# Split an expert table in two and gather its halves with separate indirect transfers

## The chip, the cores and the metric

The kernel runs on one core of one Trainium2 chip. The metric is device time of one execution in microseconds (us); the kernel before takes 2918.26 us (median of 3 runs, 2916.95 to 2922.1).

## The reference

Two transformer blocks run one after the other on one sequence of 512 tokens of width 1024, all in float32. The change lies in the last layer of the second block, a mixture of very small experts. Each of 16,384 experts is one pair of vectors of 1024 numbers: a down vector `u` and an up vector `v`. Each token picks 16 experts in each of 8 heads.

```
def peer(h, w_query, keys_1, keys_2, expert_u, expert_v):
...
    def chunk_fn(hc):
...
        top_s, pos = lax.top_k(cand, PEER_TOPK)
        experts = jnp.take_along_axis(cand_idx, pos, axis=-1)
        gate = jax.nn.softmax(top_s.astype(jnp.float32), axis=-1).astype(hc.dtype)
        u = jnp.take(expert_u, experts, axis=0)
        act = jax.nn.gelu(jnp.einsum('chkd,cd->chk', u, hc))
        v = jnp.take(expert_v, experts, axis=0)
        return jnp.einsum('chk,chkd->cd', gate * act, v)
```

## The kernel before

Every engine has its own program, written out by hand, and they meet at semaphores. The 512 tokens are four tiles of 128. The first 1572 us are the first block and the dense part of the second; nothing of them is touched. The expert layer follows. It runs through 32 steps (`STEPS`: 4 tiles times 8 heads) of 16 rows each (`TOPK`), 512 rows `g` in all. In row `g`, each of the 128 partitions holds the chosen expert of its own token.

- **GpSimd (POOL)** issues one indirect DMA for each row (L1662). It reads 128 expert numbers from a column of `ecur` and brings 128 table rows of 8 KB, `u` and `v` side by side, into slot `g % RING` of `ring_e`, a ring of 10 slots in the `arena`. For a step's first row it waits for `ecur_ready`, and from row 10 on for `rows_used`, which says that TensorE is done with the slot. Nothing else stands on this queue in this stage.
- **VectorE (DVE)** waits for the row's own semaphore `row_landed`, and forms the dot product of `u` with the token's vector (`row_dot`, L1581). This is a custom instruction that reads two operands in SBUF, and it writes the product over `u`. Between two dots it does one of 16 pieces of routing for the step after next (`route`): these find the top 16 of the candidates and end with `ecur`.
- **ScalarE (ACT)** takes the dots two at a time (`weigh_pair`): Gelu (L1041), the gate (L1045), and two diagonal matrices `diag` (L1047, L1049).
- **TensorE (PE)** multiplies each diagonal by the `v` half of its slot, two matmuls of 128x512 a row, accumulated over a tile's 128 rows in PSUM (`row_pair`; matmuls are recorded at L415), and adds 1 to `rows_used` after each row.
- Between rows of the first tile TensorE also does the query projections and key scores of the steps to come, whose weights come on SyncE's queue in rows of 4 KB. At the end of each tile its sum is turned and added to `x` (`turn_tile`, `add_tile`).

The ring is what couples the engines: a slot's journey is issue, DMA queue, transfer, dot, weighing, matmul, release, and there are 10 slots.

The `v` half lies behind the `u` half in a slot (elements `D` to `2D`). The one semaphore of a row says that both have landed.

Of the kernel before, what the change touches and what calls it, by code (L numbers as in the profile page):

```python
# [20 lines left out]
D = 1024  # L21
# [82 lines left out]
def build(nc, a, out):  # L104
    ctx = ExitStack()
    with ctx:
# [214 lines left out]
        pm_ready = sem("pm_ready")  # L321
        pn_ready = sem("pn_ready")
        pool_done = sem("pool_done")
        pool_seen = sem("pool_seen")
        pq_done = sem("pq_done")
        prep_done = sem("prep_done")
        prep_ps = sem("prep_ps")
# [30 lines left out]
        ug_ready = sem("ug_ready")  # L358
        uw_done = sem("uw_done")
        vc_ready = sem("vc_ready")  # L360
        vec_seen = sem("vec_seen")
        vec_step = sem("vec_step")
        vnew_ready = sem("vnew_ready")
        w_ready = sem("w_ready")
# [10 lines left out]
        slot_ready = [sem(f"slot{j}_ready") for j in range(SLOTS)]  # L375
        slot_a_ready = [sem(f"ada_slot{j}_ready") for j in range(SLOTS)]
        slot_2_ready = [sem(f"ada_2_slot{j}_ready") for j in range(SLOTS)]
        row_landed = [sem(f"expert_row{j}_ready") for j in range(RING)]

        block = ctx.enter_context(nc.Block())  # L380

# [31 lines left out]
        def _(pe):  # L413
# [316 lines left out]
            def row_pair(p, start, stop):  # L730

                pe.wait_ge(diag_ready, p + 1)
                c = p // (HEADS * SB)
                for k in range(BATCH):
                    r = (p * BATCH + k) % RING
                    for v in range(2):
                        ins = mm(PS[:, 4 * (c % 2) + v, :], diag[:, p % NB, k, :],
                                 ring_e[:, r, D + v * S:D + (v + 1) * S],
                                 start and k == 0, stop and k == BATCH - 1)
                    ins.then_inc(rows_used, 1)  # L740
# [366 lines left out]
        def _(dve):  # L1107
# [386 lines left out]
            def route(r, j):  # L1494
# [25 lines left out]
                elif j == 5:  # L1520
                    copy(idf, icur[:]).then_inc(vec_step, 1)
                    tt(cand.rearrange("p (x y) -> p x y", y=16), last(vcur[:, 0, :], 16), mid(vcur[:, 1, :], 16), ADD).then_inc(vec_step, 1)
                    n(vec_step), n(vec_step)
                elif j == 6:
                    V.max(tcur[:, 0:8], cand).then_inc(vec_step, 1)
                    n(vec_step)
                elif j == 7:
                    V.max_index(pcur[:, 0:8], tcur[:, 0:8], cand).then_inc(vec_step, 1)
                    n(vec_step)
                elif j == 8:  # L1530
                    V.match_replace(s2, tcur[:, 0:8], cand, NEG).then_inc(vec_step, 1)
                    n(vec_step)
                elif j == 9:
                    V.max(tcur[:, 8:16], s2).then_inc(vec_step, 1)
                    n(vec_step)
                elif j == 10:
                    V.max_index(pcur[:, 8:16], tcur[:, 8:16], s2).then_inc(vec_step, 1)
                    n(vec_step)
                elif j == 11:
                    V.tensor_scalar(pab[:, 0, :], pcur[:], 4, None, ALU.logical_shift_right).then_inc(vec_step, 1)  # L1540
                    V.tensor_scalar(pab[:, 1, :], pcur[:], 15, None, ALU.bitwise_and).then_inc(vec_step, 1)
                    n(vec_step), n(vec_step)
                elif j == 12:
                    copy(ifl, pab[:]).then_inc(vec_step, 1)
                    n(vec_step)
                    settled()
                    tt(eqv, last(ifl, 16), mid(iota, 2, 16), ALU.is_equal).then_inc(vec_step, 1)
                    n(vec_step)
                elif j == 13:
                    tt(eqv, eqv, idf.unsqueeze(2).to_broadcast([P, 2, 16, 16]), MUL).then_inc(vec_step, 1)  # L1550
                    n(vec_step)
                elif j == 14:
                    V.tensor_reduce(sel.rearrange("p z k -> p (z k)"), eqv.rearrange("p z k x -> p (z k) x"), X, ADD).then_inc(vec_step, 1)
                    n(vec_step)
                else:
                    stt(exf, sel[:, 0, :], float(NKEYS), sel[:, 1, :], MUL, ADD).then_inc(vec_step, 1)
                    n(vec_step)
                    if r >= 3:
                        dve.wait_ge(w_ready2, (r - 2) * TOPK)
                    tt(gcur[:, r % 3, :], tcur, tcur[:, 0:1].to_broadcast([P, 16]), SUB).then_inc(sm_in, 1)  # L1560
                    settled()
                    copy(ecur[:, r % 2, :], exf).then_inc(ecur_ready, 1)

            def gate_sum(r):
# [73 lines left out]
        def _(pool):  # L1638
# [17 lines left out]
            for r in range(STEPS):  # L1656
                pool.wait_ge(ecur_ready, r + 1)
                for j in range(TOPK):
                    g = r * TOPK + j
                    if g >= RING:  # L1660
                        pool.wait_ge(rows_used, g - RING + 1)
                    nc.gpsimd.indirect_dma_start(  # L1662
                        out=ring_e[:, g % RING, :], out_offset=None, in_=a["experts"],
                        in_offset=bass.IndirectOffsetOnAxis(ap=ecur[:, r % 2, j:j + 1], axis=0)
                    ).then_inc(row_landed[g % RING], 16)


def tiles_of(w):
# [50 lines left out]
def layout(i):  # L1719
# [20 lines left out]
    order = np.array([0, 1, 2, 3, 4, 8, 5, 9, 6, 10, 7, 11] + list(range(12, 28)))  # L1740
    a["w_in_2"] = np.ascontiguousarray(tiles_of(g["w_in_2"][0])[order])
    a["branch"] = np.ascontiguousarray(np.concatenate([tiles_of(g["pool_up_2"][0]), tiles_of(g["conv_out_2"][0])], 2))
    a["experts"] = np.concatenate([g["expert_u_2"][0], g["expert_v_2"][0]], 1)
    m = np.zeros((P, NMATS), np.float32)
    for n, v in (("w2k", g["cmp_k_w2"][0]), ("w2v", g["cmp_v_w2"][0]), ("keys1", g["sub_keys_1_2"][0].T),
                 ("keys2", g["sub_keys_2_2"][0].T), ("poolw", g["pool_w_2"][0].transpose(1, 0, 2).reshape(P, -1))):
# [43 lines left out]
```

## Time and profile before

| | |
|---|---|
| median of 3 runs | 2918.26 us |
| profiled execution's own time | 2921.43 us |
| its span, first to last instruction | 2919.7 us |
| mean granted TensorE clock, of full speed | 0.938 |
| busy: PE, DVE, ACT, POOL | 2474.1, 1579.5, 677.9, 597.0 us |
| moved by the GpSimd queue | 587.24 MB in 87,552 packets |
| first indirect issue to last | 1572.4 to 2877.2 us |

The busy times are over the whole span. The expert layer is its last 1350 us, and there each engine stands differently than in the mean, so the views are read by stretches of time. "DMA share" is the mean busy share of the core's 16 DMA engines. The records of packets overlap a little, so that it can read 1.01.

### The profile page before, as it was taken

Reading aid. Unit: us, or ns where it says so; the run is one execution under the profiler, and the core shown is the slowest. Engines: PE = TensorE matmul, PEld = TensorE weight load, DVE = VectorE, ACT = ScalarE, POOL = GpSimd, SP = SyncE. Lnnn points to the kernel's source line nnn. Section 1 sums busy time; section 2 is a strip of 40 time slices with the busy share of each in tenths; the row PEclk is TensorE's granted clock in tenths of the full one; section 3 lists DMA queues with packets and bytes.
Section 4 is the critical chain, followed back from the end, with each engine's and each line's share of the span. In section 5 each row is a group of like instructions: output and inputs, shape, how many; then the busy total and the mean of one; then the engine's idle time right before and its main releaser. Section 6 shows DMA issues by size and latency. Waiting matters only on the chain.

```text
span 2919.7 us, 21725 instructions
## 1 busy us (share of the span) xinstructions
PE 2474.1 (85%) x6738; PEld 1189.6 (41%) x6738; DVE 1579.5 (54%) x3290; ACT 677.9 (23%) x1886; POOL 597.0 (20%) x612
## 2 busy tenths in 40 slices
PE   4998697788999999899898999787777777777776
PEld 3442496653444454344344444233333323232233
DVE  4731774433665500357314666667666766667664
ACT  2112121312010000211102333333333333333332
POOL 1100000000000000000001444444444444344441
PEclk7998696799999989999899999999999999999999
DMA  6541001012443311122124899999999999999995
GB/s 243 187 151 36 0 0 36 22 58 87 165 155 139 136 60 65 57 79 72 49 74 194 352 407 404 421 421 421 421 421 420 421 422 421 403 421 422 421 421 243
DMA packets 115590, 682.61 MB, mean 234 GB/s; under 512 B 12446, under 2 KB 16542, under 8 KB 49708
## 3 DMA queue, kind: packets, MB, share of 16 engines
q0 software_dynamic: 87552, 587.24, 49.4%
q1 hardware_dynamic: 27948, 94.29, 9.4%
q8 instruction: 42, 0.69, 0.1%
q14 instruction: 48, 0.39, 0.0%
HBM read 679.39 MB, written 2.10 MB: 233 GB/s over the span
## 4 chain that ended last, share of the span: by engine, by line
PE 50%; DMA 25%; DVE 5%; ACT 4%; issue 1%; POOL 1%; DVEq 0%; ACTq 0%; POOLq 0%
PE PS L415 49%; DMA arena<-experts_dram,ecur 25%; DVE arena L1581 2%; DVE arena L1112 1%; ACT arena L1045 1%; POOL arena L1662 1%; ACT L1041 1%; ACT const L1049 0%; ACT const L1047 0%; DVE arena L1359 0%; DVE rs L1165 0%; ACT arena L1041 0%; PE PS L628 0%; DVE arena L1118 0%; DVE arena L1115 0%
## 5 line engine op out<-in xcount | busy, mean ns | idle before, releaser
L415 PE MATMUL PS<-arena,const 128*128 128x512 f32 (+1 forms) x2076 | 981.1, 620 | 279.8 <-ACT const L1049 262.1
L1581 DVE CUSTOM_DVE_ANT_0 arena<-arena 128x1024 f32<-128x1024 f32 x512 | 627.4, 1225 | 422.0 <-DMA arena<-experts_dram,ecur 420.5
L1662 POOL DMA_INDIRECT arena<-experts_dram,ecur x512 | 546.0, 1066 | 1349.0 <-PE PS L415 735.0
L415 PE MATMUL PS<-hT,ring 128*128 128x512 f32 x1792 | 784.6, 597 | 22.7 <-ACT hT L832 22.0
L415 PEld LDWEIGHTS PS<-arena,const 128*128 128x128 f32 x2076 | 390.6, 196 | 852.1 <-issue 434.5
L415 PEld LDWEIGHTS PS<-hT,ring 128*128 128x128 f32 x1792 | 341.8, 192 | 449.9 <-issue 444.3
L415 PE MATMUL PS<-arena,ring 128*128 128x512 f32 (+1 forms) x864 | 352.4, 574 | 18.5 <-ACT arena L999 11.5
L415 PEld LDWEIGHTS PS<-arena,ring 128*128 128x128 f32 x864 | 170.0, 215 | 201.0 <-issue 183.6
L1041 ACT ACTIVATE arena<-arena 128x2 f32<-128x2 f32 x256 | 51.8, 202 | 711.1 <-DVE arena L1581 710.7
L415 PE MATMUL PS<-arena 128*128 128x128 f32 (+2 forms) x1216 | 182.0, 314 | 23.3 <-DVE arena L1112 8.7
L415 PEld LDWEIGHTS PS<-arena 128*128 128x128 f32 x1216 | 166.3, 215 | 42.2 <-issue 17.3
L1118 DVE SCALAR_TENSOR_TENSOR xT<-PS,mod,xT 128x128 f32<-128x128 f32 (+1 forms) x56 | 29.2, 522 | 273.6 <-PE PS L415 265.3
L1112 DVE TENSOR_TENSOR arena<-arena 128x16 f32<-128x16 f32 (+6 forms) x190 | 98.4, 518 | 97.0 <-ACT arena L976 48.9
L1118 DVE SCALAR_TENSOR_TENSOR arena<-arena,silc 128x512 f32<-128x512 f32 (+1 forms) x168 | 126.3, 752 | 12.7 <-DMA arena<-ada_dram 7.0
L1045 ACT ACTIVATE arena<-arena 128x1 f32<-128x1 f32 x512 | 122.8, 287 | 8.6
L1115 DVE TENSOR_SCALAR arena<-PS,param 128x512 f32<-128x512 f32 x56 | 44.6, 797 | 134.0 <-PE PS L415 130.7
L824 ACT ACTIVATE sq<-xT 128x512 f32<-128x512 f32 x32 | 20.1, 630 | 368.6 <-PE PS L415 202.2
L1118 DVE SCALAR_TENSOR_TENSOR arena<-PS,param,arena 128x511 f32<-128x511 f32 (+2 forms) x124 | 92.9, 749 | 14.4 <-DVE arena L1115 1.8
L1047 ACT ACTIVATE const<-const,arena 128x128 f32<-128x128 f32 x256 | 98.8, 386 | 0.0
L1049 ACT ACTIVATE const<-const,arena 128x128 f32<-128x128 f32 x256 | 98.7, 386 | 0.0
L415 PE MATMUL PS<-sq,const 128*128 128x512 f32 (+2 forms) x174 | 70.2, 555 | 30.0 <-ACT sq L824 14.8
L1647 POOL DMA_DIRECT2D arena<-ada_dram x4 | 2.1, 528 | 452.0 <-ACT arena L950 452.0
(171 smaller groups left out, 1335.0 us busy)
## 6 DMA issues: line engine op xcount, KB each, us to landing
arena<-ada_dram POOLq DMA_DIRECT2D x96, 512.0 KB, 5.0
ring<-w_in_dram SPq DMA_DIRECT2D x52, 512.0 KB, 3.5
ring<-up_dram SPq DMA_DIRECT2D x44, 512.0 KB, 3.5
ring<-down_dram SPq DMA_DIRECT2D x16, 704.0 KB, 4.0
ring<-w_out_dram SPq DMA_DIRECT2D x16, 512.0 KB, 3.5
ring<-query_dram SPq DMA_DIRECT2D x16, 512.0 KB, 5.6
arena<-experts_dram,ecur POOLq DMA_INDIRECT x512
ring<-cmp_dram SPq DMA_DIRECT2D x8, 512.0 KB, 3.5
```

Of the source, the lines that this page charges most:

```text
L415: return nc.tensor.matmul(o, l, r, start=start, stop=stop)
L824: A(sq[:, k % 2, :], xT[:, k, :], ACT.Square).then_inc(sq_ready, 1)
L1041: A(wts[:, b, :], dots[:, b, :], ACT.Gelu_apprx_tanh).then_inc(gelu_ready, 1)
L1045: A(wts[:, b, k:k + 1], wts[:, b, k:k + 1], ACT.Copy, scale=gcur[:, r % 3, j:j + 1]).then_inc(w_ready2, 1)
L1047: A(diag[:, b, 0, :], ident, ACT.Copy, scale=wts[:, b, 0:1]).then_inc(act_step, 1)
L1049: A(diag[:, b, 1, :], ident, ACT.Copy, scale=wts[:, b, 1:2]).then_inc(diag_ready, 1)
L1112: return V.tensor_tensor(out=o, in0=x, in1=y, op=op)
L1115: return V.tensor_scalar(o, x, s1, s2, op0, op1)
L1118: return V.scalar_tensor_tensor(out=o, in0=x, scalar=s_, in1=y, op0=op0, op1=op1)
L1581: V.tensor_tensor_reduce(out=u, in0=u, in1=hrow[:, (r // HEADS) % 2, :], scale=1.0, scalar=0.0, op0=MUL, op1=ADD, accum_out=dots[:, p % NB ...
L1647: pool.dma_start(ring_2[:, j, :], a["ada_2"][j]).then_inc(slot_2_ready[j], 16)
L1662: nc.gpsimd.indirect_dma_start(out=ring_e[:, g % RING, :], out_offset=None, in_=a["experts"], in_offset=bass.IndirectOffsetOnAxis(ap=ecur[ ...
```

## The change

The table `experts` (16,384 rows of 8 KB) becomes two tables, `expert_u` and `expert_v` (rows of 4 KB). For each row `g` GpSimd issues two indirect DMAs with the same indices, the `u` half first, each with a semaphore of its own in each slot: `row_landed` for `u`, the new `v_landed` for `v`. VectorE's dot waits for `u` alone. TensorE waits for `v` before a row's matmuls. The bytes that are moved stay the same, and so do the ring and the order of the rows.

```
         row_landed = [sem(f"expert_u{j}_ready") for j in range(RING)]
+        v_landed = [sem(f"expert_v{j}_ready") for j in range(RING)]
...
                 for k in range(BATCH):
-                    r = (p * BATCH + k) % RING
+                    g = p * BATCH + k
+                    r = g % RING
+                    pe.wait_ge(v_landed[r], 16 * (g // RING + 1))
...
                     settled()
+                    if r >= 2:
+                        for g in range((r - 2) * TOPK, (r - 1) * TOPK):
+                            dve.wait_ge(v_landed[g % RING], 16 * (g // RING + 1))
                     copy(ecur[:, r % 2, :], exf).then_inc(ecur_ready, 1)
...
                     nc.gpsimd.indirect_dma_start(
-                        out=ring_e[:, g % RING, :], out_offset=None, in_=a["experts"],
+                        out=ring_e[:, g % RING, :D], out_offset=None, in_=a["expert_u"],
                         in_offset=bass.IndirectOffsetOnAxis(ap=ecur[:, r % 2, j:j + 1], axis=0)
                     ).then_inc(row_landed[g % RING], 16)
+                    nc.gpsimd.indirect_dma_start(
+                        out=ring_e[:, g % RING, D:], out_offset=None, in_=a["expert_v"],
+                        in_offset=bass.IndirectOffsetOnAxis(ap=ecur[:, r % 2, j:j + 1], axis=0)
+                    ).then_inc(v_landed[g % RING], 16)
```

The first place is GpSimd's queue at the head of the expert layer, where it turned to the gathers. Before, from the last instructions of the loop that loads the modulation weights (`x9` is nine such rows one after the other):

```order
L1648 COMPARE_AND_BRANCH
L1662 DMA arena<-experts_dram,ecur 128x2048 [waits ecur_ready]
L1662 DMA arena<-experts_dram,ecur 128x2048 x9
L1662 DMA arena<-experts_dram,ecur 128x2048 [waits rows_used] x6
L1662 DMA arena<-experts_dram,ecur 128x2048 [waits rows_used,ecur_ready]
L1662 DMA arena<-experts_dram,ecur 128x2048 [waits rows_used] x15
```

After the change, on the same engine, from the last row of the ring's first filling to the second step's first row:

```order
L1666 DMA arena<-expert_u_dram,ecur 128x1024
L1670 DMA arena<-expert_v_dram,ecur 128x1024
L1666 DMA arena<-expert_u_dram,ecur 128x1024 [waits rows_used]
L1670 DMA arena<-expert_v_dram,ecur 128x1024
...
L1666 DMA arena<-expert_u_dram,ecur 128x1024 [waits rows_used,ecur_ready]
L1670 DMA arena<-expert_v_dram,ecur 128x1024
```

Each issue has become two, 1024 instead of 2048 elements in a partition, and only the first of the two waits. The queue holds 1024 gathers where it held 512.

The second place is VectorE at the end of a step, where `ecur` of the step after next is written. Before (the ISA rows are the dot and the reading of its accumulator):

```order
L1553 TENSOR_REDUCE arena<-arena 128x32 [waits vec_step]
L1581 ISA arena<-arena 128x1024 [waits expert_row1_ready]
L1581 ISA arena 128x1
L1118 SCALAR_TENSOR_TENSOR arena<-arena 128x16 [waits vec_step]
L1112 TENSOR_TENSOR arena<-arena 128x16 [waits w_ready2]
L1121 CAST ecur<-arena 128x16 [waits vec_step]
L1581 ISA arena<-arena 128x1024 [waits expert_row2_ready]
```

After, at the same place:

```order
L1554 TENSOR_REDUCE arena<-arena 128x32 [waits vec_step]
L1585 ISA arena<-arena 128x1024 [waits expert_u1_ready]
L1585 ISA arena 128x1
L1119 SCALAR_TENSOR_TENSOR arena<-arena 128x16 [waits vec_step]
L1113 TENSOR_TENSOR arena<-arena 128x16 [waits w_ready2]
L1122 CAST ecur<-arena 128x16 [waits expert_v4_ready,expert_v3_ready,expert_v5_ready,expert_v2_ready,expert_v6_ready,expert_v1_ready,expert_v7_ready,expert_v0_ready,expert_v8_ready,expert_v9_ready,vec_step]
L1585 ISA arena<-arena 128x1024 [waits expert_u2_ready]
```

No instruction has moved. The cast that gives GpSimd its next numbers now also waits until the `v` halves of the step just done, its last row among them, have landed, since those transfers read the `ecur` that it overwrites. On TensorE the matmul rows stand as before, and the first matmul of each row names `expert_v`*n*`_ready` as a further wait.

## Rows read from the trace of the kernel before

**Rows 1.** Windows: busy us (instructions) by engine, clock, DMA share, GB/s
```profile
1572.00:1600.00 28.00, 28.00 (x91) 14.37 (x90) 10.11 (x40) 5.78 (x10) 9.46 (x10) 1.00 0.94 380
1600.00:1700.00 100.00, 96.70 (x257) 45.33 (x256) 64.88 (x172) 36.67 (x117) 37.76 (x33) 1.00 0.91 366
1700.00:1800.00 100.00, 100.00 (x264) 46.70 (x263) 63.59 (x161) 34.33 (x112) 42.45 (x40) 1.00 0.99 398
1800.00:1900.00 100.00, 75.41 (x167) 30.61 (x166) 68.97 (x178) 34.95 (x114) 44.65 (x40) 0.96 1.01 422
1900.00:2880.00 980.00, 750.64 (x1634) 301.97 (x1634) 661.98 (x1641) 321.98 (x1078) 411.68 (x390) 0.97 1.01 420
```

**Rows 2.** Chain that ended last, in time order, from 1995 to 2030 us
```profile
2001.95 1.25 DVE arena L1581 x2
...
2004.57 3.71 PE PS L415 x8
...
2008.55 18.23 DMA arena<-experts_dram,ecur
...
2026.80 1.24 DVE arena L1581 x2
```

**Rows 3.** DMA view, 2000 to 2200 us: gathers alone
```profile
DMA packets 11569, 84.26 MB, mean 421 GB/s; under 512 B 1286, under 2 KB 1286, under 8 KB 1286
```

**Rows 4.** DMA view, 38 to 44 us: weights in rows of 4 KB
```profile
DMA packets 679, 2.45 MB, mean 408 GB/s; under 512 B 82, under 2 KB 82, under 8 KB 679
```

**Rows 5.** Windows of 2 us in that stretch, columns as in Rows 1
```profile
38.00:40.00 2.00, 0.01 (x1) 0.00 (x0) 1.97 (x2) 0.00 (x0) 0.00 (x0) 0.50 1.00 401
40.00:42.00 2.00, 0.00 (x0) 0.00 (x0) 1.90 (x4) 0.00 (x0) 0.00 (x0) 0.50 1.05 420
```

**Rows 6.** The issuing line: its group on the page, then 1700 us to the end
```profile
L1662 POOL DMA_INDIRECT arena<-experts_dram,ecur x512 | 546.0, 1066 | 1349.0 <-PE PS L415 735.0
```
```profile
L1662 POOL DMA_INDIRECT arena<-experts_dram,ecur x470: 932/937/1993, 1699.4 to 2877.2; - x157
```

**Rows 7.** Timeline of POOL while the ring fills: start, us, [idle before <-releaser]
```profile
1574.94 0.94 POOL L1662 DMA_INDIRECT arena<-experts_dram,ecur  x1 [0.30 <-issue]
1576.18 0.94 POOL L1662 DMA_INDIRECT arena<-experts_dram,ecur  x1 [0.30 <-issue]
```

**Rows 8.** Timeline of POOL, 2060 to 2069 us
```profile
2061.27 0.94 POOL L1662 DMA_INDIRECT arena<-experts_dram,ecur  x1 [1.56 <-PE PS L415]
2062.99 1.62 POOL L1662 DMA_INDIRECT arena<-experts_dram,ecur  x1 [0.78 <-PE PS L415]
2064.92 0.94 POOL L1662 DMA_INDIRECT arena<-experts_dram,ecur  x1 [0.30 <-issue]
```

**Rows 9.** Timeline of DVE, the same stretch: dots
```profile
2062.58 1.23 DVE L1581 CUSTOM_DVE_ANT_0 arena<-arena 128x1024 f32<-128x1024 f32 x1 [0.70 <-DMA arena<-experts_dram,ecur]
...
2065.06 1.22 DVE L1581 CUSTOM_DVE_ANT_0 arena<-arena 128x1024 f32<-128x1024 f32 x1 [0.83 <-DMA arena<-experts_dram,ecur]
```

**Rows 10.** Waits from 1700 to 2880 us: in total, times, longest
```profile
POOL arena L1662 <- PE PS L415: 660.8, 423, 8.7
```

**Rows 11.** The page's GB/s in 40 equal slices of 73 us
```profile
GB/s 243 187 151 36 0 0 36 22 58 87 165 155 139 136 60 65 57 79 72 49 74 194 352 407 404 421 421 421 421 421 420 421 422 421 403 421 422 421 421 243
```

**Rows 12.** Timeline of all engines at the end of a step
```profile
2008.27 0.17 DVE L1121 CAST ecur<-arena 128x16 uint32<-128x16 f32 x1
...
2009.40 1.23 DVE L1581 CUSTOM_DVE_ANT_0 arena<-arena 128x1024 f32<-128x1024 f32 x1 [0.96 <-DMA arena<-experts_dram,ecur]
...
2009.54 3.70 PE L415 MATMUL PS<-arena,const 128*128 128x512 f32 x8 [1.26 <-ACT const L1049]
```

**Rows 13.** Chain that ended last, at the end of the gathers
```profile
2877.19 18.13 DMA arena<-experts_dram,ecur
...
2895.34 1.24 DVE arena L1581 x2
...
2897.96 5.49 PE PS L415 x24
```

More of the change, by code:

```diff
@@ L323, in build @@
         pool_done = sem("pool_done")
-        pool_seen = sem("pool_seen")
         pq_done = sem("pq_done")
@@ L360, in build @@
         vc_ready = sem("vc_ready")
-        vec_seen = sem("vec_seen")
         vec_step = sem("vec_step")
@@ L377, in build @@
         slot_2_ready = [sem(f"ada_2_slot{j}_ready") for j in range(SLOTS)]
-        row_landed = [sem(f"expert_row{j}_ready") for j in range(RING)]
+        row_landed = [sem(f"expert_u{j}_ready") for j in range(RING)]
+        v_landed = [sem(f"expert_v{j}_ready") for j in range(RING)]
         block = ctx.enter_context(nc.Block())
@@ L1742, in layout @@
     a["branch"] = np.ascontiguousarray(np.concatenate([tiles_of(g["pool_up_2"][0]), tiles_of(g["conv_out_2"][0])], 2))
-    a["experts"] = np.concatenate([g["expert_u_2"][0], g["expert_v_2"][0]], 1)
+    a["expert_u"], a["expert_v"] = np.ascontiguousarray(g["expert_u_2"][0]), np.ascontiguousarray(g["expert_v_2"][0])
     m = np.zeros((P, NMATS), np.float32)
```

## The prediction

> **What bounds the kernel now.** Read the windows first [rows 1]. From 1800 to 2880 us the DMA share stands at 1.01 and the rate at 420 to 422 GB/s, while TensorE is busy 77% (750.64 of 980 us), VectorE 68% and GpSimd 42%. The 16 DMA engines have no idle time left in that stretch; every other engine has. The chain of waits says the same: of each turn of the ring of 25 us, some 18 us are the wait for a gather to land [rows 2]. At 421 GB/s [rows 3] a row of 128 x 8192 B = 1.0486 MB takes 2.49 us, so those 18 us are mostly seven older rows in the DMA queue, and not latency. The dots start when a row lands, 2.48 us apart [rows 9]. Ahead of 1800 us it is otherwise: in the first tile the query projections keep TensorE busy 97 to 100%, and the DMA share is 0.91, then 0.99.
>
> So the price of this change is read from what a row costs the DMA engines, and then from whether GpSimd can still feed them.
>
> **DMA: the same bytes in packets of half the size.** Before, a row is 128 packets of 8 KB and 16 small ones for the semaphore: in [rows 3] 1286 of 11,569 packets are under 512 B, one in nine. After, it is 256 packets of 4 KB and 32 small ones. No gather of 4 KB rows is in the trace, but weights in rows of 4 KB are, and at 38 to 44 us two queues of them keep the DMA engines as full: 679 packets, 82 of them small, all others under 8 KB, 408 GB/s [rows 4]. At 408 GB/s a row takes 2.57 us, 0.08 us more than 2.49. In single windows of 2 us there the rate is 401 and 420 GB/s at shares of 1.00 and 1.05 [rows 5]. These are my bounds: 2.50 us (+0.01) and 2.615 us (+0.125). I take the mean over the stretch, since it is the longest full one of such packets.
>
> The Trainium skill ("DMA: Bandwidth & Descriptors", Why small descriptors are slow) gives a cost for each packet of about 3 cycles beside one cycle for each 32 B, and a little metadata. By that rule 4 KB packets would cost 1.2 to 1.5% more than those of 8 KB, an estimate from the page of +14 to +18 us here. The rows say 421/408, or 3.2%, and the sum goes by them.
>
> How many rows pay it? 470 of the 512 issues start after 1699 us [rows 6]. The 42 before fall where the DMA engines idle: 9% of 100 us are 9 us against 33 x 0.08 = 2.6 us, so they pay nothing. Without that cover it would be 42 x 0.08 = 3.4 us. The 40 rows from 1700 to 1800 us find 1% idle, 1 us. That makes 470 x 0.08 - 1 = **+36.6 us**.
>
> **GpSimd: two issues for one.** While the ring fills, issues stand back to back: 0.94 us and a gap of 0.30, 1.24 us each [rows 7], and two are 2.48 us a row against the DMA engines' 2.57. That leaves almost nothing, and issues are not always 0.94 us: the mean is 1.066 [rows 6]. The long ones have one look. The issue at 2062.99 took 1.62 us: a dot ran from 2062.58 to 2063.81, and the issue ended 0.80 us after it [rows 8, 9]. An issue that starts during a dot is held until the dot ends and then needs 0.8 us; one that starts first isn't held, as at 2064.92, 0.14 us before the next dot.
>
> From that I work out whether GpSimd keeps up when it is behind. Dots come every 2.57 us and last 1.23. An issue held until a dot's end is done 0.81 us later; the next starts 1.11 us after the dot's end, and the next dot only 2.57 - 1.23 = 1.34 us after it. So this second issue goes through in 0.94 us, and the third starts 2.35 us after the dot's end, within the next dot, and is held to its end. Two issues for each dot: just enough. I put the steady state at **0**. The margin is 0.23 us, and what is once lost isn't regained while the dots come at that pace.
>
> Where is it lost? At the end of a tile TensorE frees no slot for up to 8.7 us [rows 10] and then several at once. Now GpSimd refills at 1.24 us a row, twice as fast as the DMA engines drain. Even so the slice at 2482 to 2555 us shows 403 GB/s for 421 [rows 11], 4.3% of 73 us = 3.1 us lost at the third boundary, and none at the other two. With 2.48 us a row the queue isn't refilled, so I let all three boundaries lose that: **+6 us**. Bounds: 0, and 3 x 8.7 = 26 us.
>
> **The new waits.** A wait already satisfied costs GpSimd nothing that shows: the gap of 0.30 us stands at 2064.92 too, where the instruction has one [rows 7, 8]. VectorE's cast into `ecur` now waits for the last `v` of the step. In a full queue that `v` lands 1.3 us after its `u`, about when the dot of 1.23 us ends, and VectorE idles 0.96 us before the next dot [rows 12]. Behind the cast stands that dot; if the cover is gone, 32 casts at up to 1.3 us are 42 us at most. TensorE's wait for `v`: its matmuls start over 2.5 us after a pair's second dot begins (2001.95 to 2004.57, [rows 2]), `v` is there, and TensorE idles 1.26 us before a pair [rows 12]. Only up to 1800 us has it no idle time: some 75 rows, at 0.05 us each below 4 us. I take 0 for all of these.
>
> **The gain.** The last dot waits for the last `u` and no longer for the last byte: the chain there is transfer, dot from 2895.34, matmuls from 2897.96 [rows 13], and the dot starts half a row earlier, **-1.3 us**. At the head, the first dots wait for nothing that a gather brings late. Within the full stretch an earlier `u` only frees slots sooner, and the queue is seven rows deep already.
>
> **Sum**: 2921.4 (the profiled execution's own time) + 36.6 + 0 + 6 + 0 - 1.3 = 2962.7 us. That execution lies 3.2 us above the median of 2918.3, so the forecast for a median is **2960 us**.
>
> **Rivals.**
> - *GpSimd becomes the bound.* For it: 2 x (1.066 + 0.30) = 2.73 us a row from the means as they are [rows 6, 7], 0.24 more than 2.49: + 470 x 0.24 = 113 us, **3030 us**. If issues and dots met at random, 1.23 of 2.57 us would find a dot running with 0.61 us still to go, 0.29 us for each issue, 2 x (1.24 + 0.29) = 3.06 us a row: +268 us, 3186 us. Against it: the two fall into step as worked out, and a held issue is held only because it would otherwise be early. It decides once an issue takes more than 2.57/2 - 0.30 = 0.985 us in the mean without the hold being such spare time. The Trainium skill ("SBUF — State Buffer", Who interferes with whom) has the rule: a VectorE instruction with two SBUF inputs contends with a GpSimd instruction that reads SBUF, and the second to start is blocked. The trace agrees, 1.62 us for 0.94.
> - *No change.* 4 KB packets run at the 420 GB/s of the better window and GpSimd keeps up: 470 x 0.01 = 5, less 1.3: **2922 us**. For it: two windows of 2 us are little to tell 401 from 420.
> - *Faster.* The dot starts 1.3 us earlier after its issue, slots turn sooner, and the DMA idle time up to 1800 us (6% of 28, 9% of 100, 1% of 100: 12 us) goes with the 1.3 us at the end: **2905 us**. It needs packets of 4 KB at no cost, as above; and there TensorE, busy 97 to 100%, is the bound. An earlier `u` doesn't help it.
>
> The skill's rules for kernel authors on the same DMA page advise one large transfer over several. Its fit of about 2 us fixed for each DMA would add 2 us a row if nothing overlapped; rows landing 2.48 us apart show that it overlaps.
>
> **Chances.** My forecast, the packets' price with GpSimd in step: 0.50. GpSimd the bound: 0.35. No change: 0.10. Faster: 0.05. A measurement of this kernel can tell 0.2%, about 6 us, so the first two are slower (0.85). The range goes from 2930, which leaves out the last two, to 3130, into the upper part of the first rival; the forecast's own cases, from the better bound to the worse (470 x 0.125 = 59 us), lie between 2925 and 2985.
>
> **What would show it.** After the change, from 1800 us on: DMA share still 1.00 to 1.01 at 408 GB/s, dots 2.57 us apart, GpSimd busy 80% and more with issues of 0.94 and about 1.05 us in turn, and VectorE's idle time still ended by the gather of `u`. If the share falls below 0.97 while GpSimd's idle time before an issue is 0.30 us throughout and no longer ended by TensorE, GpSimd is the bound. If the rate is 420, the packets cost nothing. The forecast fails above all if the step of two issues a dot is lost in places and not found again, or if the cast's wait holds VectorE.

## The result and the profile after

The changed kernel takes 3100.64 us (median of 4 runs, 3096.23 to 3103.57) against 2919.22 us before (2916.95 to 2922.1, 4 runs beside them): ratio 1.062, 95% interval 1.0601 to 1.0638. That is slower, by 181 us where 41 were forecast.

The windows of the kernel after, with the columns of [rows 1]:

```profile
1600.00:1700.00 100.00, 96.70 (x252) 45.17 (x251) 63.22 (x169) 35.80 (x114) 63.34 (x62) 0.98 0.88 330
1700.00:1800.00 100.00, 93.19 (x238) 42.52 (x237) 58.95 (x149) 30.75 (x101) 72.41 (x68) 0.98 0.97 365
1800.00:1900.00 100.00, 73.64 (x154) 30.69 (x153) 57.74 (x145) 27.78 (x94) 75.11 (x71) 0.91 0.96 364
1900.00:3050.00 1150.00, 819.62 (x1668) 333.68 (x1666) 676.55 (x1686) 331.65 (x1107) 859.54 (x793) 0.89 0.97 363
```

From 1900 us on the DMA share is 0.97 and the rate 363 GB/s, where 1.00 at 408 was forecast. So two things are off: the DMA engines have gaps, and even at a full share the rate would be 363/0.97 = 374 GB/s. GpSimd is busy 75% and does 793 issues in 1150 us, 2.90 us a row.

The page of the kernel after: the DMA rate in 40 slices of 77 us, and the two issuing lines:

```profile
GB/s 230 199 134 21 0 0 55 1 82 156 156 155 140 56 70 54 75 75 55 54 236 381 361 379 347 372 364 362 374 334 371 353 378 362 362 349 373 356 372 271
...
L1666 POOL DMA_INDIRECT arena<-expert_u_dram,ecur x512 | 513.8, 1004 | 828.9 <-DVE ecur L1122 587.1
...
L1670 POOL DMA_INDIRECT arena<-expert_v_dram,ecur x512 | 588.3, 1149 | 156.0 <-issue 155.4
```

Where [rows 11] holds 421, slice after slice, the rate now goes up and down between 334 and 381. The two issues of a row take 1.004 + 1.149 us in the mean and 0.30 in front of each, 2.75 us. At first sight this is the rival in which GpSimd is the bound, with its 2.73 us a row. The waits say that this isn't all. Waits of the kernel after, 1700 to 3050 us (in total, times, longest); "remote" stands where no record of a signal explains the release:

```profile
POOL arena L1666 <- remote: 40.2, 20, 4.5
POOL arena L1666 <- PE PS L414: 38.9, 44, 6.9
ACT arena L1058 <- remote: 33.7, 4, 17.6
ACT arena L1018 <- remote: 25.6, 3, 11.6
DVE xT L1119 <- remote: 17.9, 4, 6.7
DVE arena L1571 <- issue: 15.6, 2, 15.3
```

The trace of the kernel before has no wait that ends with "remote" in this stretch. One such place, timeline of the kernel after in the last step but one of the second tile:

```profile
2284.30 1.04 PE L725 MATMUL PS<-const,hT 128*128 128x128 f32 x8
...
2298.29 0.60 ACT L1058 ACTIVATE arena<-PS 128x512 f32<-128x512 f32 x1 [17.58 <-remote]
...
2303.36 0.16 DVE L1571 RECIPROCAL arena<-arena 128x1 f32<-128x1 f32 x1 [15.28 <-issue]
...
2305.99 3.78 PE L414 MATMUL PS<-arena,const 128*128 128x512 f32 x4 [20.65 <-ACT const L1050]
```

TensorE's eight transposes, which turn the token rows of the next tile (`turn_rows`), begin at 2284.30 and take 1.04 us of work. ScalarE, whose next work waits for them alone, copies their result 13 us later. VectorE then waits for ScalarE and TensorE for both, and the three stand for 15 to 21 us. GpSimd has the same at smaller scale, 20 times up to 4.5 us.

### The profile page after: what moved, and what is told of

It is laid out like the page before. It is cut to its first block, busy times and chain, and to the rows that moved or that the text cites. A ratio compares the mean times of both kernels' runs of the same rounds, so it can differ in the third digit from the quotient of the medians.

```text
span 3094.5 us, 22733 instructions
## 1 busy us (share of the span) xinstructions
PE 2534.9 (82%) x6738; PEld 1216.9 (39%) x6738; DVE 1578.0 (51%) x3290; ACT 677.5 (22%) x1886; POOL 1153.4 (37%) x1124
## 4 chain that ended last, share of the span: by engine, by line
PE 52%; POOL 12%; issue 11%; DVE 4%; DMA 3%; another core or an unknown queue 2%; ACT 2%; POOLq 0%; DVEq 0%; ACTq 0%
PE PS L414 51%; POOL arena L1670 6%; POOL arena L1666 5%; DMA arena<-expert_u_dram,ecur 3%; DVE arena L1585 1%; DVE arena L1113 1%; ACT arena L1046 0%; DVE arena L1360 0%; DVE rs L1166 0%; PE PS L627 0%; ACT const L1050 0%; DVE xT L1119 0%; ACT const L1048 0%; DVE arena L1119 0%
## 5 line engine op out<-in xcount | busy, mean ns | idle before, releaser
L414 PE MATMUL PS<-arena,const 128*128 128x512 f32 (+1 forms) x2076 | 1044.3, 656 | 392.5 <-issue 260.8
L1666 POOL DMA_INDIRECT arena<-expert_u_dram,ecur x512 | 513.8, 1004 | 828.9 <-DVE ecur L1122 587.1
L414 PEld LDWEIGHTS PS<-arena,const 128*128 128x128 f32 x2076 | 419.7, 209 | 999.5 <-issue 849.3
L1670 POOL DMA_INDIRECT arena<-expert_v_dram,ecur x512 | 588.3, 1149 | 156.0 <-issue 155.4
L1651 POOL DMA_DIRECT2D arena<-ada_dram x4 | 2.1, 530 | 447.3 <-ACT arena L951 447.3
L1656 POOL DMA_DIRECT2D arena<-ada_dram x44 | 23.3, 530 | 333.3 <-DVE arena L1119 333.3
L1048 ACT ACTIVATE const<-const,arena 128x128 f32<-128x128 f32 x256 | 98.8, 386 | 0.0
```

The source lines that it names most:

```text
L414: return nc.tensor.matmul(o, l, r, start=start, stop=stop)
L1048: A(diag[:, b, 0, :], ident, ACT.Copy, scale=wts[:, b, 0:1]).then_inc(act_step, 1)
L1656: pool.dma_start(ring_2[:, j, :], a["ada_2"][bass.ds(i * SLOTS + j, 1)].rearrange("o p n -> p (o n)")).then_inc(slot_2_ready[j], 16)
L1666: nc.gpsimd.indirect_dma_start(out=ring_e[:, g % RING, :D], out_offset=None, in_=a["expert_u"], in_offset=bass.IndirectOffsetOnAxis(ap=ecu ...
L1670: nc.gpsimd.indirect_dma_start(out=ring_e[:, g % RING, D:], out_offset=None, in_=a["expert_v"], in_offset=bass.IndirectOffsetOnAxis(ap=ecu ...
```

## The experiments

All times are medians, and each ratio is taken against the kernel before, run on the same occasion. The experiments fell on six occasions after the first result. The kernel before stood at 2917.8 to 2919.8 us on all of them. The changed kernel did not: unedited, it has two levels.

| changed kernel, unedited | us | range, runs | ratio, interval |
|---|---|---|---|
| the result | 3100.64 | 3096.23 to 3103.57, 4 | 1.062, 1.0601 to 1.0638 |
| `r_after_again` | 2964.06 | 2949.45 to 2973.39, 4 | 1.014, 1.0101 to 1.0179 |
| `r_after_third` | 2962.57 | 2954.2 to 2976.5, 4 | 1.0157, 1.0121 to 1.0192 |
| `r_after_fourth` | 2969.35 | 2955.08 to 2991.35, 6 | 1.0177, 1.0146 to 1.0208 |
| `r_after_fifth` | 3091.89 | 3089.04 to 3101.93, 5 | 1.0593, 1.0578 to 1.0607 |
| `r_after_sixth` | 3085.65 | 3078.66 to 3113.02, 4 | 1.0607, 1.0556 to 1.0658 |

On one occasion all runs of it stand at one level. I call them the lower (2963 to 2969) and the upper (3086 to 3101). Every interval lies above 1, but only the upper level is more than 2% slower beyond doubt. The expectations of the first four experiments (`e_one_operand`, `e_v_plain`, `e_extra_gather`, `e_one_signal`) took 3100 us for the kernel's only time. Their occasion was of the lower level, so what an edit took away there is counted from some 2965 us.

### On occasions of the lower level

**`e_one_operand`: take away what holds an issue.**

```
-                V.tensor_tensor_reduce(out=u, in0=u, in1=hrow[:, (r // HEADS) % 2, :], ...
+                V.tensor_reduce(dots[:, p % NB, g % BATCH:g % BATCH + 1], u, X, ADD).then_inc(dots_ready, 1)
```

> The changed kernel, but VectorE's dot is a plain sum over u (one operand in SBUF, nothing written over u) in place of the product with the token's vector, so the output is not the reference's; issues, packets, signals and waits are as in the changed kernel. If a gather's issue is held by the two-operand dot and GpSimd is the bound: every issue takes 0.94 us, a row costs GpSimd 2.48 us, the DMA engines become the bound at 2.57 us a row, and the kernel takes about 2960 us. If the time comes from something else (packets, waits for v, late signals), issues may get shorter but the time stays within 30 us of 3100.

Measured: 2946.47 us (2945.02 to 2949.81), ratio 1.0099 (1.0082 to 1.0116), 21 us below `e_one_signal` on the same occasion (2967.86). Windows of it, then its issues from 1900 to 2850 us (count; busy us, mean ns; idle before):

```profile
1900.00:2850.00 950.00, 713.24 (x1547) 287.20 (x1545) 630.93 (x1232) 309.26 (x1028) 698.62 (x740) 0.96 1.03 409
```
```profile
L1668 POOL DMA_INDIRECT arena<-expert_v_dram,ecur x370 | 350.1, 946 | 113.1 <-issue 112.8 <-PE PS L414 0.3
L1664 POOL DMA_INDIRECT arena<-expert_u_dram,ecur x370 | 349.9, 946 | 138.6 <-issue 93.8 <-PE PS L414 44.8
```

With a dot of one SBUF operand the issues take 0.946 us in the mean, GpSimd waits for slots again, and the DMA engines run full at 409 GB/s.

**`e_one_operand_before`: the same edit in the kernel before**, as the control.

> The kernel before (one gather of 8 KB a row) with a dot that only sums u, so that it reads one operand in SBUF and leaves the product with the token out. It is the control to the same edit in the changed kernel (2946 us). If the hold of an issue by a dot costs the kernel before nothing, since its GpSimd waits for slots anyway, the time stays within 0.2% of 2919 us, and the issues' mean falls from 1.07 to 0.94 us. If the dot's own length or the hold cost something there too, it comes out 5 us or more below, and the packets' price in the changed kernel is larger than 27 us by that much.

Measured: 2914.8 us (2913.84 to 2917.39, 10 runs), ratio 0.9987 (0.9978 to 0.9996); the issues' mean is 952 ns. The dot's form is worth 3.8 us there. Between the two kernels with the short dot lie 2946.47 - 2914.8 = 31.7 us (two occasions, the kernel before at 2918.29 and 2918.61 us). With hardly an issue held in either, this is what the packets (and whatever else a second issue costs) amount to: 0.067 us for each of 470 rows.

**`e_v_plain` and `e_v_sync`: one gather a row, the packets as in the change.** The first lets GpSimd bring `v` in a plain DMA, the second SyncE.

```
+                    pool.dma_start(ring_e[:, g % RING, D:], a["expert_v"][(g % 128) * P:(g % 128 + 1) * P]
+                                   ).then_inc(v_landed[g % RING], 16)
```

> The changed kernel, but the v half comes by a plain DMA from GpSimd's queue of 128 fixed table rows of 4 KB (no indices; output not the reference's). Bytes, packets of 4 KB, number of transfers and their signals and waits are the same; a plain issue took 0.53 us in the trace of before. If GpSimd's issuing is the bound: 0.53 + 0.30 + 1.0 + 0.30 = 2.1 to 2.2 us a row, below the DMA engines' 2.57; about 2960 us with the DMA share at 1.0. If packets of 4 KB or the doubled signals are what costs, it stays near 3100 us.

Measured: 2950.29 us (2948.91 to 2952.44), ratio 1.0111 (1.0094 to 1.0128), 408 GB/s. The expectation's 1.0 us for the indirect issue was a miss: it took 1.57 us in the mean, mostly held by a dot and done 0.85 us after the dot's end. With 0.56 us for the plain issue GpSimd still kept up.

> The changed kernel, but the v half comes by a plain DMA on SyncE's queue of 128 fixed table rows of 4 KB, issued row by row as slots come free (the last four query weight blocks are issued between them; output not the reference's). GpSimd issues one gather a row, as before the change; packets of 4 KB, transfers and signals are as many as in the changed kernel, and the early dot is kept. If only the packets cost: 2.57 us a row and 2945 to 2955 us. If the early dot or the many signals slow the kernel by themselves: 3000 us and more.

Measured: 2950.87 us (2949.11 to 2952.12), ratio 1.0112 (1.0095 to 1.0128), 408 GB/s. Both say 32 us for the packets, with dots as they are and GpSimd, in `e_v_sync`, as idle as in the kernel before. In both, `v` comes from fixed table rows and not from chosen ones.

**`e_extra_gather`: the second gather without small table rows.**

```
-                        out=ring_e[:, g % RING, :D], out_offset=None, in_=a["expert_u"],
+                        out=ring_e[:, g % RING, :], out_offset=None, in_=a["experts"],
...
-                        out=ring_e[:, g % RING, D:], out_offset=None, in_=a["expert_v"],
+                        out=spare[:, g % RING, :], out_offset=None, in_=a["extra"],
```

> The gather of before (8 KB rows, one transfer) plus a second gather of 16 B per token with the same indices into a spare buffer that nobody uses (its signal is waited for as v's is). Two gathers and two signals a row, but the bytes come in packets of 8 KB. If GpSimd's issuing is the bound: as slow as the changed kernel, 3070 to 3110 us, with the DMA share clearly below 1. If packet size is what costs: about 2925 us (the 128 small packets add little).

Measured: 2958.23 us (2956.84 to 2958.48), ratio 1.0134 (1.0117 to 1.0151). Neither theory had that: 40 us with packets of 8 KB kept, far from GpSimd as the bound. Its second gather moves only 2 KB a row. Its window from 1900 us:

```profile
1900.00:2850.00 950.00, 716.73 (x1534) 289.63 (x1535) 631.35 (x1596) 304.48 (x1017) 728.09 (x729) 0.95 1.01 404
```

The DMA engines have no idle time here, and yet they move 404 GB/s where the kernel before moves 420. In nearly all stretches of 40 us outside the spells described below it is 404 to 411, as with rows of 4 KB (409 in most stretches of `e_v_sync`). Both kernels have 288 packets a row where the kernel before has 144. So most of the price is one for the number of packets and not for the size of a table row: 128 packets of 16 bytes and 16 for the signal cost here what splitting 128 packets in two costs there. The expectation's "the 128 small packets add little" was wrong.

**`e_one_signal`: the new waits and the early dot taken back.** Both halves add to one semaphore, the dot waits for both, and TensorE and the cast no longer wait for `v`.

> The changed kernel, but both halves count on one semaphore and the dot waits for both (32 instead of 16); TensorE and the cast into ecur no longer wait for v. Tells what the separate signal and its waits cost or bring. If the waits for v on TensorE or on VectorE's cast are part of the loss: 10 to 60 us below 3100. If issuing is the bound: the ring loses only 1.3 us of lead per row and the time stays at 3100 within 15 us.

Measured: 2967.86 us (2964.45 to 2972.4), ratio 1.0167 (1.015 to 1.0184), the same as the changed kernel at its lower level (2963 to 2969, on other occasions). So the separate signals cost and bring nothing that shows beside those 7 us.

**`r_after_again`: the changed kernel unedited.**

> The changed kernel itself, word for word, once more, on the chip and beside the kernels of this call. The first four experiments with the same 1024 issues took 2946 to 2968 us, the changed kernel 3100; its trace has semaphore updates of TensorE that reach their waiters up to 13 us late, and theirs do not. If that belongs to the kernel (its early dot meeting the issues), it is again 3090 to 3110 us with issues of 1.08 us in the mean. If it belongs to where it was run, it is 2950 to 2975 us here.

Measured: 2964.06 us. Its trace shows what GpSimd's two issues cost when nothing else disturbs. Its issues from 2190 to 2300 us, then from 2304 to 2483 us:

```profile
L1666 POOL DMA_INDIRECT arena<-expert_u_dram,ecur x42 | 44.8, 1067 | 12.8 <-issue 11.9 <-PE PS L414 0.9
L1670 POOL DMA_INDIRECT arena<-expert_v_dram,ecur x43 | 40.3, 936 | 13.1 <-issue 12.5 <-PE PS L414 0.6
```
```profile
L1670 POOL DMA_INDIRECT arena<-expert_v_dram,ecur x65 | 76.4, 1176 | 19.8 <-issue 19.8
L1666 POOL DMA_INDIRECT arena<-expert_u_dram,ecur x64 | 63.8, 997 | 19.5 <-issue 17.1 <-PE PS L414 2.4
```

And the windows of it, one in step and the two that hold the spells out of step (2304 to 2483 and 2648 to 2827 us), with one between them:

```profile
1900.00:2300.00 400.00, 299.38 (x658) 120.67 (x657) 265.09 (x669) 127.14 (x429) 306.05 (x309) 0.97 1.02 405
2304.00:2483.00 179.00, 134.42 (x265) 53.59 (x266) 114.87 (x288) 55.28 (x183) 139.84 (x129) 0.90 1.00 380
2490.00:2640.00 150.00, 115.97 (x261) 47.76 (x260) 98.38 (x249) 47.30 (x160) 114.51 (x117) 0.95 1.02 407
2648.00:2827.00 179.00, 129.56 (x264) 51.67 (x262) 114.30 (x287) 53.98 (x180) 140.06 (x128) 0.92 0.99 377
```

In step, one of the two issues is 1.067 us and the other 0.936: two for each dot, as worked out. Out of step both are held at times, 1.176 + 0.997 + 0.60 = 2.77 us a row, and the rate is 380 and 377 GB/s for 406: 179 x (1 - 380/406) + 179 x (1 - 377/406) = 24 us lost. How a spell looks, timeline of GpSimd and the dots:

```profile
2659.78 2.28 DVE L1119 SCALAR_TENSOR_TENSOR xT<-PS,mod,xT 128x128 f32<-128x128 f32 x6
...
2662.64 1.21 DVE L1585 CUSTOM_DVE_ANT_0 arena<-arena 128x1024 f32<-128x1024 f32 x1
2662.70 1.96 POOL L1670 DMA_INDIRECT arena<-expert_v_dram,ecur  x1 [0.30 <-issue]
...
2664.19 1.22 DVE L1585 CUSTOM_DVE_ANT_0 arena<-arena 128x1024 f32<-128x1024 f32 x1
2664.96 1.26 POOL L1666 DMA_INDIRECT arena<-expert_u_dram,ecur  x1 [0.30 <-issue]
...
2665.68 1.21 DVE L1585 CUSTOM_DVE_ANT_0 arena<-arena 128x1024 f32<-128x1024 f32 x1
2666.53 1.17 POOL L1670 DMA_INDIRECT arena<-expert_v_dram,ecur  x1 [0.30 <-issue]
```

The first line is the last six of the eight instructions of `add_tile`, which adds the finished tile's sum to `x`. In all they take VectorE 3.05 us, from 2659.01, and rows land meanwhile. The dots then stand 1.5 us apart, since VectorE catches up with them, and three issues in a row are held, each to 0.8 us after a dot's end (2663.85 + 0.81 = 2664.66). The forecast's two issues a dot took dots at even distances.

The seven traces of the lower level with two gathers a row and the long dot (`r_after_again`, `r_after_third`, `r_after_fourth`, `e_one_signal`, `e_v_first`, `e_one_table`, `e_extra_gather`) all have `add_tile` at 2314 to 2321 us and again at 2652 to 2665. From 2280 to 2320 us their rate is 402 to 409 GB/s, from 2320 to 2360 it is 372 to 383; from 2680 to 2720 it is 368 to 392. `e_one_operand` has `add_tile` too, at 2311 and 2643 us, and there the rate stays at 410. So a spell needs issues that dots can hold, and it begins where `add_tile` has bunched the dots. The first `add_tile`, near 1984 us, brings a smaller fall or none, and no run leaves `add_tile` out. How long a spell lasts differs, from some 40 us in `r_after_third` to some 180 here.

**`e_v_first`: `v` issued before `u`**, so that the dot is late instead of early.

> The changed kernel with the two issues of a row exchanged: v first, then u. The dot now waits for the row's last byte, as before the change, and v is always there. Issues, packets, signals are the same. If what GpSimd loses above the packets' 2.57 us a row is a matter of where the dots fall between the issues: still 2950 to 2975 us, with stretches of steps at 2.56 us and others at 2.75 us a row. If the early dot is what brings dots and issues out of step: 2950 us throughout.

Measured: 2971.35 us (2963.29 to 2974.88), ratio 1.0175 (1.0152 to 1.0197), beside `r_after_third`:

> The changed kernel itself a third time. It took 3100 us in the first comparison and 2964 us (2949 to 2973) in the second, with the kernel before at 2919 both times. If the first was a matter of that place or time, this is 2945 to 2975 us again, without late semaphore updates. If the kernel has two ways to run, 3100 us can come back, here or within the rounds.

at 2962.57 us. The rate falls at the same places. The order of the halves is no cause of the spells.

**`e_more_signals`: `e_v_sync` with three more tiny transfers a row**, since the upper level's trace shows late signals:

```
+                for x in range(3):
+                    sp.dma_start(spare[0:16, g % RING, x, :], a["extra"][0:16]).then_inc(v_landed[g % RING], 16)
```

> The kernel with v by SyncE's plain DMAs, and behind each of them three tiny ones (16 x 16 B) on the same semaphore, which TensorE and the cast wait for with 64 in place of 16 (output not the reference's). A row has five transfers' signals in place of the changed kernel's two and the kernel before's one; GpSimd has one issue a row. If many signals are what makes semaphore updates arrive late: well above 3000 us, with updates of TensorE late in the trace. If not: 2950 to 2990 us.

Measured: 2980.77 us (2979.3 to 2982.22), ratio 1.0209 (1.0192 to 1.0226), no wait that ends with "remote". The 96 small packets that a row has more than in `e_v_sync` go with 30 us (2980.77 - 2950.87, two occasions), and signals in number make none late, at least on an occasion of the lower level.

**`r_after_fourth`, and `e_one_table`: the table not split**, its rows 2e and 2e + 1 gathered.

```
-                        in_offset=bass.IndirectOffsetOnAxis(ap=ecur[:, r % 2, j:j + 1], axis=0)
+                        in_offset=bass.IndirectOffsetOnAxis(ap=ecur[:, r % 2, TOPK + j:TOPK + j + 1], axis=0)
```

> The changed kernel once more, nothing edited, with five rounds. Of four medians of it so far one stood at 3100 us and the later ones at 2964 and 2963. If the 3100 us are a place or a time and not the kernel's, as I now hold, it comes out at 2955 to 2975, issues of 1.00 to 1.04 us in the mean, TensorE's semaphore updates at the end of the matmul. If the kernel itself has such a way of running, so that it should come back now and then, 3090 to 3110, with DMA share near 0.97 at 363 GB/s and updates up to 13 us late.

> The changed kernel, but the table isn't split: u and v of an expert stand side by side as before, and the two gathers of a row read the 4 KB rows 2e and 2e+1 of it (VectorE writes 32 numbers a step instead of 16, in two instructions where one stood). If what a row costs more comes from the packets' size and GpSimd's two issues alone, 2955 to 2975 us, as the changed kernel beside it. If it comes from where the halves stand in the memory (two tables, each with its own region), most of it goes, 2925 to 2940 us.

The first expectation counts one median too many: there were three. Measured: 2969.35 us, and 2972.71 us (2963.9 to 2984.07), ratio 1.0193 (1.0175 to 1.021). Where the halves stand in memory makes no difference that shows at the lower level.

### On occasions of the upper level

**`r_after_fifth` and `r_one_operand_again`.** Their chip is the one on which `e_one_operand` and `e_one_signal` had stood at the lower level.

> The changed kernel again, on whatever chip it falls to, with its one-operand form beside it. If 3100 us belong to a place, most places give 2955 to 2975 us, issues near 1.02 us in the mean and about 1.01 of DMA share at 396 to 400 GB/s; where 3100 comes back, the neighbour on the same chip tells what it rests on. If the first result was a rare event of one loading, it is 2955 to 2975 us here too.

> The changed kernel with a dot that only sums u (one operand in SBUF), as once before, beside the unchanged one. On a place where the changed kernel runs at 2960 us: 2944 to 2952. On a place where it runs at 3100: 2944 to 2952 as well if all the loss there comes from held issues; 3000 to 3030 if signals that come late stop the ring there whatever the dot reads.

Measured: 3091.89 us for the changed kernel, and 3072.44 us (3069.19 to 3082.78) with the short dot, ratio 1.0532 (1.0511 to 1.0553); that is more than the expectation had for late signals. Waits of the latter, 1700 us to the end:

```profile
POOL arena L1664 <- PE PS L414: 125.9, 53, 5.5
...
POOL arena L1664 <- remote: 56.8, 20, 5.1
...
ACT arena L1018 <- remote: 35.2, 4, 11.9
DVE xT L1119 <- remote: 23.6, 3, 11.9
```

Hardly an issue is held in it, they take 0.94 us in the mean, and GpSimd waits 183 us for slots (54 in `e_one_operand`, to 2850 us); still 126 us of the loss stay (3072.44 - 2946.47). Its DMA rate from 2000 to 2200 us, in slices of 5 us:

```profile
GB/s 415 405 407 412 177 347 393 416 410 303 362 418 409 377 266 312 384 415 413 410 409 410 208 326 382 417 410 410 410 410 303 245 333 403 417 410 410 410 406 206
```

`e_one_operand` holds 406 to 411 in every slice of the same stretch. Here the engines reach that rate too, and most of the loss lies in six stops. The hold is worth 19.5 us here (3091.89 - 3072.44) and 16 to 23 at the lower level (2962.57 to 2969.35, less 2946.47). So the upper level isn't the time that dots hold GpSimd's issues: it is 126 us of something else, on top.

**`r_after_sixth`, `r_v_sync_again`, `r_extra_again`, one after the other on one chip.** The count in the first expectation is one too many: there were three low medians of the unedited kernel, and the fourth is that of `e_one_signal`, which is also the low one on the same chip.

> The changed kernel once more, as the measure for three others beside it. Of six medians so far two stood at 3092 and 3101 us and four at 2963 to 2969 (one of the low ones and one of the high ones on the same chip, so it isn't the chip). I expect one of the two again, 2955 to 2975 or 3085 to 3105, and nothing between; the three others tell what the high one rests on only if it comes.

> As e_v_sync: v comes by SyncE's plain transfers from fixed rows, and GpSimd issues one gather a row (the sum is over other rows of v). Where the changed kernel stands at 2965, 2951 as before. Where it stands at 3100: 2951 as well if the late signals come from GpSimd's second gather of each row, 3060 or more if they come from the doubled number of packets and landing signals, which this kernel has too.

> As e_extra_gather: u and v in one gather of 8 KB rows, and a second gather of 16 B rows into a buffer that nobody reads, waited for as v is. Where the changed kernel stands at 2965, 2958 as before. Where it stands at 3100: 3060 or more if the late signals come from the second gather, 2958 if they need packets of 4 KB.

Measured: 3085.65 us; 2952.19 us (2950.59 to 2954.92), ratio 1.012 (1.0103 to 1.0136); and 3099.21 us (3088.84 to 3106.22), ratio 1.061 (1.0586 to 1.0634). Waits of `r_v_sync_again`, 1700 to 2900 us:

```profile
POOL arena L1676 <- PE PS L424: 675.0, 420, 8.7
...
POOL arena L1676 <- issue: 19.7, 46, 2.2
```

And of `r_extra_again`:

```profile
POOL spare L1671 <- issue: 124.5, 408, 0.4
POOL arena L1667 <- issue: 106.0, 348, 0.3
POOL arena L1667 <- PE PS L415: 62.0, 47, 13.1
ACT arena L1059 <- remote: 56.1, 5, 21.6
```

With all of the change's packets and landing signals but one gather a row, the time is that of the lower level (2950.87 in `e_v_sync`, the same kernel), and no wait from 1700 us on ends with "remote"; one of 2.1 us does before, the only one in a trace with one gather a row. With the table's rows left at 8 KB and a second gather of 16 bytes a partition, the upper level is there in full, ScalarE's wait for the transposes of token rows up to 21.6 us. `e_extra_gather` is the same kernel at 2958.23 us. So the upper level needs an occasion on which it can come, and on this one it came with GpSimd's second gather of each row; packets of 4 KB aren't needed for it, and with doubled landing signals alone it didn't come.

## Why the prediction was wrong

**What failed** is the step "GpSimd: two issues for one", where the prediction put "the steady state at 0". The second gather of each row on GpSimd costs 133 us at the upper level (3085.65 - 2952.19, against as many packets with one gather), and about 13 at the lower (2964.06 - 2950.87). The recorded result stands at the upper level, 140 us above the forecast. At the lower level the forecast of 2960 us is 3 to 9 us low, and that is partly luck: it had some 5 us too many for packets and too few for what stands behind the tile boundaries.

The prediction also took the DMA queue to stay "seven rows deep". With two issues a row it doesn't: in `r_after_again` a gather lands 6.6 us after its issue (median, on its page), in `e_v_sync` 18.1. Before the change a pause of GpSimd or of a slot was covered by the queue; after it, little is.

**The likely rival was not it either.** GpSimd as the bound had 3030 us, from 2.73 us a row, and the trace's 2.75 looks like it. But a row took 2.90 us, and with the hold gone the upper level keeps 126 us of its loss (`r_one_operand_again`). The longer issues in that trace are mostly not what sets its pace. The rival's second price has an error of its own: an issue that a dot holds for 0.61 us and then needs 0.81 is 0.48 us longer than 0.94, not 0.61. That makes 2.94 us a row and some 3130 us in place of 3186.

**DMA packets, +36.6 us.** Slightly large: 31.7 us with the short dot in both kernels, 32 with one gather a row, at the 408 GB/s that was forecast and a share of 1.02. The forecast tied it to the packets' size; `e_extra_gather` ties most of it to their number. The estimate from the Trainium skill ("DMA: Bandwidth & Descriptors", Why small descriptors are slow) was 14 to 18 us; the rows of weights were the better guide.

**In step.** Right as a mechanism: 1.067 and 0.936 us in turn for the forecast's 1.05 and 0.94. "What is once lost isn't regained while the dots come at that pace" was wrong in its second half: in `r_after_again` spells end after some 180 us. The hold is there with a dot of two SBUF operands and gone with one, 0.946 us. That is as the Trainium skill has it ("SBUF — State Buffer", Who interferes with whom). The short dot also writes nothing over `u`, and no run tells the two apart. All of it is worth about 19 us.

**Tile boundaries, +6 us.** Mis-sized, and for another reason than the one given. The loss isn't TensorE's pause at the boundary but the spells behind it: in `r_after_again` TensorE turns the second tile's sum at 2308 us and the third's at 2651, `add_tile` follows at 2316 and 2659, and the spells with it. They cost 24 us in that profile, within the bounds of 0 to 26.

**New waits, 0.** Right at the lower level: `e_one_signal` has none of them and is no faster. At the upper level it was not tried.

**The gain, -1.3 us.** Too small to be seen. Taking the early dot away (`e_one_signal`, `e_v_first`) changed nothing measurable.

**What stays open** is what the upper level is made of. Shown is where it shows: signals that engines wait for come many us late and part of their records is missing. It came with two gathers a row on GpSimd, on 3 of 7 occasions, and not by the chip alone; that it stays away with one rests on `r_v_sync_again`, on one occasion, and on the kernel before, on all of them. Not told apart are the second gather as such and a GpSimd that is left without spare time (675 us of waiting in `r_v_sync_again`, 62 in `r_extra_again`); `e_v_plain`, with one gather, one plain transfer and 70 us of waiting for slots in 950, ran only at the lower level. Nor is it known why, with the long dot, packets take longer there even at a full share (363/0.97 = 374 GB/s against 396/1.01 = 392).

## What to carry to other kernels

Where a DMA queue is the bound, splitting its transfers costs the packets' price (some 3% of a row from 144 to 288 packets here) and then whatever the issuing engine runs into: count its time per row against the bound, and treat a margin of a few per cent as none. An issue that is held behind another engine's work stays in step only while that work comes evenly, and a queue that was deep before is thin once its issuer is near its limit. And a time from one occasion may be a level and not the kernel's only one: repeat a surprising one elsewhere, with a neighbour that lacks the suspect, before explaining it.

## What the runs showed of the hardware

- An indirect gather of 128 rows that isn't held occupies GpSimd for 0.94 to 0.95 us, with 0.30 us ahead of it where issues stand back to back, whether the rows are 8 KB, 4 KB or 16 bytes. One that starts within a dot of two SBUF operands, written over one of them, ends 0.8 us after it; beside sums of one operand the mean is 0.946 us.
- At a full DMA share the expert rows came at 421 GB/s with 144 packets a row and at about 409 with 288, whether the packets were 4 KB long or half of them 8 KB and half 16 bytes.
- The same kernel had two levels 4% apart, each steady over all runs of an occasion, while the kernel before stood at 2918 to 2920 us beside it. On one chip the kernel with the short dot stood at 2946.47 us once and at 3072.44 later. Beside the kernel before, four kernels were run where it showed; the three with two gathers a row had it, the one with one gather had not.
- At the upper level ScalarE took up a result of TensorE 13 us after it was due, at the end of a wait of 17.6 us; the longest wait for the same transposes was 21.6 us in `r_extra_again`, 7.1 in `r_after_sixth`, and 4.3 at the lower level.
